# Shift pieces of the opening, issued on TensorE two at a time behind the third and the fifth piece of a round

## What is computed

```python
mod = silu(c) @ w_ada + b_ada                 # 2048 -> 3 * 2048
shift, scale, gate = split(mod, 3)
h = rms_norm(x, norm_g) * (1 + scale) + shift # (256, 2048)
proj = h @ w_in                               # 2048 -> 13824
...                                           # three branches (pool, attention, conv) and their gates
x = x + gate * (merged @ w_out)
return rms_norm(x, final_g)
```

## Time and profile before

| | |
|---|---|
| time, median of 3 | 961.99 us (961.75 to 963.5) |
| time of the profiled execution | 964.44 us |
| its span in the trace | 961.5 us |
| PE busy | 918.0 us, 95% |
| DVE busy | 683.3 us, 71% |
| ACT busy | 417.8 us, 43% |

### The profile page before, as it was taken

One profiled execution on the slowest core, in us unless ns is written; L12 is line 12 of the kernel. 1 busy time (PEld: TensorE's weight loads), 2 busy tenths in 40 slices (PEclk: granted clock), 3 DMA queues, 4 the chain that ended last, 5 costly groups with the idle time before them and its releaser, 6 DMA issues.

```text
span 961.5 us, 10327 instructions
## 1 busy us (share of the span) xinstructions
PE 918.0 (95%) x4259; PEld 743.9 (77%) x4259; DVE 683.3 (71%) x782; ACT 417.8 (43%) x375; POOL 10.0 (1%) x27
## 2 busy tenths in 40 slices
PE   1599999999999999999999999999999999999996
PEld 0477777777888888888888888888888888887884
DVE  3665777848969777776778776585677878755653
ACT  2527251644344333434465655347433433434332
POOL 2000000000000000000000000000000000000000
PEclk9699999999999999999999999999999999999998
DMA  9999898864546655656535454554779998965512
GB/s 327 382 346 387 316 385 324 297 215 137 170 132 218 197 197 182 211 177 195 196 132 169 139 168 129 185 175 145 253 247 389 374 330 302 316 199 201 175 44 87
DMA packets 107757, 220.00 MB, mean 229 GB/s; under 512 B 3664, under 2 KB 3744, under 8 KB 106944
## 3 DMA queue, kind: packets, MB, share of 16 engines
q1 hardware_dynamic: 106304, 212.88, 64.5%
q0 software_dynamic: 1120, 5.43, 1.5%
q10 hardware_dynamic: 288, 1.05, 0.3%
HBM read 217.25 MB, written 2.10 MB: 228 GB/s over the span
## 4 chain that ended last, share of the span: by engine, by line
PE 92%; DMA 3%; DVE 2%; ACT 2%; issue 1%; SPq 0%; DVEq 0%; ACTq 0%
PE acc_even L1055 13%; PE acc_odd L1055 13%; PE acc_odd L1057 13%; PE acc_odd L1056 13%; PE acc_even L1057 13%; PE acc_even L1056 13%; PE side_a L1055 2%; PE side_a L1057 2%; PE side_a L1056 2%; DMA raw<-in_w_in 2%; DMA raw<-in_w_ada 1%; PE side_b L1085 1%; PE side_b L1199 1%; PE side_b L1055 1%; ACT wh L419 1%
## 5 line engine op out<-in xcount | busy, mean ns | idle before, releaser
L649 DVE TENSOR_TENSOR wl<-raw,wh 128x2048 fp32r<-128x2048 f32 x152 | 347.6, 2290 | 198.0 <-ACT wh L419 197.7
L419 ACT ACTIVATE wh<-raw 128x2048 fp32r<-128x2048 f32 x152 | 289.8, 1913 | 285.8 <-PE acc_even L1057 114.7
L1055 PE MATMUL acc_even<-wh,act_h 128*128 128x512 f32 x432 | 172.7, 400 | 8.0 <-DVE act_l L705 5.2
L1055 PE MATMUL acc_odd<-wh,act_h 128*128 128x512 f32 x432 | 170.0, 393 | 0.7 <-DVE part_u L721 0.7
L1057 PE MATMUL acc_even<-wh,act_l 128*128 128x512 f32 x432 | 169.4, 392 | 0.0
L1056 PE MATMUL acc_even<-wl,act_h 128*128 128x512 f32 x432 | 169.2, 392 | 0.0
L1057 PE MATMUL acc_odd<-wh,act_l 128*128 128x512 f32 x432 | 168.3, 390 | 0.0
L1056 PE MATMUL acc_odd<-wl,act_h 128*128 128x512 f32 x432 | 168.1, 389 | 0.0
L1055 PEld LDWEIGHTS acc_even<-wh,act_h 128*128 128x128 f32 x432 | 81.8, 189 | 27.5 <-issue 6.4
L795 DVE SCALAR_TENSOR_TENSOR conv_slots<-conv_slots,taps 128x256 f32<-128x256 f32 x240 | 100.2, 479 | 0.2
L1055 PEld LDWEIGHTS acc_odd<-wh,act_h 128*128 128x128 f32 x432 | 81.1, 188 | 18.4 <-DVE part_u L721 1.1
(11 more groups left out here) (265 smaller groups left out, 893.2 us busy)
## 6 DMA issues: line engine op xcount, KB each, us to landing
raw<-in_w_in SPq DMA_DIRECT2D x108, 1024.0 KB, 5.1
raw<-in_w_ada SPq DMA_DIRECT2D x48, 1024.0 KB, 7.7
raw<-in_w_out SPq DMA_DIRECT2D x16, 1024.0 KB, 5.0
raw<-in_w_branch_pool SPq DMA_DIRECT2D x8, 1024.0 KB, 5.0
raw<-in_w_branch_attn SPq DMA_DIRECT2D x8, 1024.0 KB, 5.0
raw<-in_w_branch_conv SPq DMA_DIRECT2D x8, 1024.0 KB, 6.9
raw<-in_conv_pw SPq DMA_DIRECT2D x4, 1024.0 KB, 5.1
x_tok<-in_x SPq DMA_DIRECT2D x1, 2048.0 KB, 8.6
```

The costliest lines, as they stand in the source:

```text
L419: nc.scalar.activation(wh[:, m % RING], raw[SLOT_OF[g]][:, :, :], ACT.Copy).then_inc(high_done, 1)
L649: nc.vector.tensor_tensor(wl[:, m % RING], raw[SLOT_OF[load_of(m)]][:, :, :], wh[:, m % RING].bitcast(F32), ALU.subtract).then_inc(raw_don ...
L1055: nc.tensor.matmul(sums, xh, wh[:, slot, i, :], start=begin, stop=False)
```

## The change

The four shift pieces of a round stood behind pieces 1, 2, 3 and 4, one at each. Now shift 0 and shift 1 stand behind piece 2, and shift 2 and shift 3 behind piece 4. Only PE's order changes; the list of loads, the buffers and the orders of DVE, ACT, SP and POOL stay.

```diff
--- before.py
+++ after.py
@@ -1145,7 +1145,8 @@
                         piece(act_h, act_l, PK * k, m, sums_of(OPEN[j]), k == 0, False)
                     else:
                         halves(m)
-                    if 1 <= j < 5:
+                    if j in (2, 4):
+                        shift_piece(k + 1, j - 2)
                         shift_piece(k + 1, j - 1)
                     if j == 5:
                         modulation(k + 1)
```

## The result

The changed kernel took 973.14 us (median of 4, 972.26 to 973.9) where the kernel before took 962.75 (median of 4, 961.75 to 964.11): a ratio of 1.0107, with a 95% interval from 1.0089 to 1.0124, so about 10 us slower. The forecast was 967.0, slower by 5.0, and its range ended at 970.5: right in direction and in where PE waits, half the size. Over the study the full change was timed 20 times, between 969.0 and 973.9. One execution of the study (in e11, 1062.46 us) ran at a clock of 0.85 from end to end and enters no median here.

What follows compares the result with a forecast made beforehand. PE's instruction stream was taken as the bound, busy nearly throughout the opening. Waits of 5.2 (rounds 1 and 2) and 1.8 (round 0) less 2.0 saved gave +5.0 us, 961.99 to 967.0; range 963.5 to 970.5.

Steps and rivals of the forecast that it cites:

- What the change saves, 0.33 a pair: On PE in the opening, two shift pieces in a row cost 2.05 instead of 2.38 us; 6 pairs, 2.0 us saved.
- The load of shift 2 held back, scale 2 and W5 behind it: In SP's load list, shift 0 ends about 5.4 us later, so these three loads go out that much later.
- the slower first transfer: First load on an idle queue: 6.15 instead of 5.0 us; each wait 1.2 us longer, sum 3.5 us higher.
- PE waits 2.5 us: In the middle of piece 4, rounds 1 and 2, PE waits for add_part 3 behind scale 2; 5.2 us for both.
- 1.8 us together: Round 0's PE waits on late loads: 0.3 for shift 3, 0.6 at piece 5, 0.9 at piece 6.
- One hiccup of a microsecond in the transfers: Behind the waits of rounds 1 and 2 slack is thin; such a delay adds up to 1 us in a round.
- The clock falls in a wait (0.13): PE's clock halves in a 2.6 us opening wait, costing up to 3.7 us each; once gives 970.7 us; chance 0.13.
- twice: PE's clock falls in two of the opening's waits: +12.4 us, 974.4 us; part of the 0.13 chance.
- One of the thin slacks behind the waits breaks too: Slack behind the opening's waits gives out: +1 us in each round, 969.5 us; chance 0.05.
- Half as long: The opening's PE waits come but half as long: +1.5 us, 963.5 us; chance 0.12.
- no waits: No PE waits added in the opening, only the saving: -2.0 us, 960.0 us; chance 0.05.
- The pure saving: The pairs' 2.0 us gained on PE without any added wait: 960.0 us; chance 0.05.

Runs made afterwards that it cites:

- e11: Full change with half a piece multiplied twice in all three rounds to fill PE's added waits; 970.79 us, ratio 1.0082 to the kernel before.
- e5: Full change, but shift 0 and 1 as a pair behind piece 1, shift 2 and 3 behind piece 4; 961.12 us against 963.27 before, ratio 0.9981.
- e3: Full change, but each scale load stands ahead of its shift load in the opening's list; 964.14 us against 963.34 before, ratio 1.0009.
- e10: Full change, but shift 0 alone behind piece 2 and shift 1 alone behind piece 3; 972.67 us against 962.80 before, ratio 1.0101.
- e6: Full change, but shift 0 and 1 behind piece 3, shift 2 and 3 behind piece 4; 991.63 us in one execution, about +28 against before.
- the first trace: Profile of one execution of the full change's first run, unaltered; 973.9 us, against 964.44 us for the profiled kernel before.
- e4: Full change, but DVE takes out piece 3's sums ahead of scale piece 2 in rounds 1 and 2; 971.86 us against 963.34 before, ratio 1.0089.
- e2: Second pair alone: full change, but shift 0 back behind piece 1 and shift 1 behind piece 2; 962.39 us against 963.34 before, ratio 0.999.
- e9: Full change, but shift 0 and 1 behind piece 1, shift 2 and 3 behind piece 3; 964.57 us against 962.80 before, ratio 1.0018.
- e13: Full change with half a piece multiplied twice in all three rounds to fill PE's added waits, again; 971.45 us, ratio 1.0094 to the kernel before.
- e14: Kernel before with 36 extra matmuls, half a piece multiplied twice in each of three rounds; 970.15 us against 962.83 unaltered, ratio 1.008.
- e1: First pair alone: full change, but shift 2 back behind piece 3 and shift 3 behind piece 4; 970.26 us against 963.34 before, ratio 1.0072.
- e7: Full change run again, unaltered; 971.52 us, ratio 1.0084 to the kernel before.
- e8: Full change with the first half of piece 4 multiplied twice in rounds 1 and 2 to fill PE's waits; 971.0 us, ratio 1.0084 to before.
- e12: Full change run again, unaltered; 972.28 us, ratio 1.0085 to the kernel before.
- e15: Full change run again, unaltered; 972.62 us, ratio 1.0095 to the kernel before.

## Why the prediction came out half

- **What the change saves, 0.33 a pair: right.** 1.85 us in the trace; e5 gets 2 us for six pairs. In round 0 the second pair didn't form, since PE waited between its two pieces: 0.3 lost that I had counted.
- **The load of shift 2 held back, scale 2 and W5 behind it: right.** Issued at 65.58 for a forecast 65.2; shown as the cause by e3, with e10 and e6 beside it. DVE got scale 2 7.96, 7.89 and 7.93 us after the issue in the three rounds, for 7.73 forecast, so the slower first transfer that the prediction weighed beside its own (1.2 us more) did not occur.
- **Rounds 1 and 2, "PE waits 2.5 us": right,** 2.44 and 2.47 on the instruction named.
- **Round 0, "1.8 us together": mis-sized,** 3.03 measured. W5 came nearly as reckoned (ACT at 76.26; 75.7 forecast), but shift 3's load landed 4 us behind it, not 2.7, and all behind that came late too: 1.76 was waited for 0.3, and 1.27 at piece 6 for 0.9. "One hiccup of a microsecond in the transfers" was in my text as a slack that might break; here it hit the wait itself.
- **"The clock falls in a wait (0.13)": the step that failed.** I took PE's being busy on both sides and the unharmed waits of up to 1.0 us for evidence that 2.5 us would be harmless. The sum had nothing for it. Every trace of the full change has one or two falls, of 1.35 to 1.6 us each: 2.9 of the 4.5 us by which the first trace exceeds the forecast's 5.0. Round 0's waits (1.2) and the lost pair (0.3) are most of the rest. I had also priced a fall at up to 3.7, from a stretch that held more PE work at half clock; that my "twice", 974.4, lies near the measured 973.14 is luck, since the price was over double and other terms, round 0 above all, made up for it.
- **"One of the thin slacks behind the waits breaks too": no.** Piece 6 and the next round's first piece were on time in rounds 1 and 2 of the full change; in e4 they were not.
- **The rivals.** "Half as long" and "no waits" are out for this change. The pure saving exists, 2.1 us, if shift 1 is moved up to shift 0 rather than shift 0 down to shift 1 (e5).

The Trainium skill's rule in "TensorE: Matmul & The Clock Gate", section "HAM oscillation — how this bites in real kernels", that waits for data between groups of matmuls can halve the clock, is borne out: the falls at 91.0 and 172.9 us in the first trace lie behind or in waits of 1.27 and 2.47 us. The waits in the Trainium skill's example there are longer, some 3 to 5 us; here shorter ones were enough, though not each time. I should have let it weigh more than 0.13.

## What to carry to other kernels

Before moving a consumer, ask what its *end* releases, and count every load that stands in the same queue behind the released one, not only the load itself. When one late load feeds several waits in a row, the wait that shows up in the trace is only the last of them; taking it away moves much of the loss to the next (e4), so mend the hole in the queue. Which step to move, to group two, depends on what each one frees and when its data land: here shift 1 could be moved up to shift 0 (e5) and shift 2 down to shift 3 (e2) at no cost, while shift 0 moved down held back the queue and shift 3 moved up had to wait for its load (e9). And added waits of over a microsecond on a busy TensorE should be priced with a chance of a fall of the clock: in the four traces of the full change 16 such waits drew seven falls, 1.35 to 1.6 us each.

## What the runs showed of the hardware

**Falls of the clock behind short waits.** Between 52 and 205 us no trace without an added wait of over a microsecond shows a fall (before, e2, e5, e13, e14); with such waits there were none in e1, e3 and e9, one in e7 and e8, two in the first, e4, e10, e12 and e15, and three in e6. The shortest waits with a fall right behind them were in e4, where narrow matmuls of the modulation stand in front of a wait of 0.72 us in round 1 and 0.70 in round 2. The first:

```profile
133.95 1.03 PE L1098 MATMUL side_b<-ones,ada_sums 128*128 128x1 f32 x8
135.70 0.50 PE L1055 MATMUL side_a<-wh,act_h 128*128 128x512 f32 x1 [0.72 <-DVE wl L649]
```

```profile
136.40:139.80 3.40, 3.40 (x10) 2.62 (x9) 3.04 (x5) 3.37 (x6) 0.00 (x0) 0.51 1.05 387
```

Nearly equal waits at equal places drew a fall in one execution and none in the next, which is a part of why the times of the same kernel spread. What decides it is open.

**An instruction fetch among the loads.** The gap of 4 us between W5 and shift 3's load holds one packet of another queue (the changed kernel, DMA from 76 to 81 us; the share is of 16 engines):

```profile
q1 hardware_dynamic: 969, 1.92, 104.0%
q8 instruction: 1, 0.02, 1.4%
```

1.4% of 16 engines over 5 us is 1.1 us on one engine, about what the load is late beyond 2.7. The four traces of the full change all have such a packet in the microsecond in which W5's split starts on ACT, and in all of them shift 3's first matmul starts 3.95 to 4.11 us behind that split. In e6, where the held loads go out 5 us later, the packet comes while the first of them is under way (the window from 75 to 76 us), and the split of W5 (on ACT) and shift 3 (on PE) are 2.73 us apart:

```profile
82.28 1.91 ACT L419 ACTIVATE wh<-raw 128x2048 fp32r<-128x2048 f32 x1 [11.90 <-DMA raw<-in_w_in]
...
85.01 1.94 PE L1085 MATMUL side_b<-raw,c_wide 128*32 128x512 f32 x8 [7.20 <-DMA raw<-in_w_ada]
```

There scale 2 is late instead: DVE gets it 9.24 us after the issue (70.32 to 79.56), against 7.96 in the first trace. So the delay of 1.3 us moves with the packet. How one packet delays a whole load, by holding up a part of it for instance, no run here shows.
